# RWKV input stage: sixteen modulation pieces fetched at once, norm to mix chunk by chunk with five outputs side by side, low-rank projections in plain fp32

## What is computed

```python
mod = silu(c) @ ada_w[0] + ada_b[0]            # 6 x 1024; shift and scale are the first two
hn  = rms_norm(x, g) * (1 + scale) + shift
xx  = 0.5 * (x_prev + x_next) - hn             # neighbours of hn in the token direction
xs  = hn[:, :, None, :] + xx[:, :, None, :] * mu     # six mixes, j = 0..5
r, k, v = xs[0] @ w_rkv[0], xs[1] @ w_rkv[1], xs[2] @ w_rkv[2]       # 1024 x 1024 each
w  = tanh(xs[3] @ w1) ;  a = xs[4] @ a1 ;  g = sigmoid(xs[5] @ g1)   # low rank: 2x64, 2x64, 2x128
kk = k * k_k ;  kk = kk / max(sqrt(sum over the head of kk^2), 1e-12)
# then the bidirectional recurrence over r, w, k, v, kk, a; then 17 more stages
```

## Time and profile before

| | us |
|---|---|
| median of 3 runs | 3714.63 (3710.47 to 3714.92) |
| the profiled execution | 3717.88 |
| its span | 3716.1 |
| PE / DVE / ACT / POOL busy | 3304.6 / 1478.5 / 1139.4 / 180.1 |
| mean granted TensorE clock | 0.942 of full |
| DMA | 623.98 MB, mean 168 GB/s |

### The profile page before, as it was taken

The page is one execution under the profiler, slowest core; times in us unless marked ns, Lnnn a source line. Parts: engine busy times, 40 slices in busy tenths (PEclk is TensorE's granted clock), DMA queues, the critical chain, the costliest instruction groups (busy, mean ns, idle before and its releaser), DMA issues. The chain is left out here.

```text
span 3716.1 us, 54738 instructions
## 1 busy us (share of the span) xinstructions
PE 3304.6 (89%) x24132; PEld 2544.8 (68%) x24132; DVE 1478.5 (40%) x2702; ACT 1139.4 (31%) x1787; POOL 180.1 (5%) x338
## 2 busy tenths in 40 slices
PE   4778887899899779997999988999989998898898
PEld 3767766555499664544777765777767876777898
DVE  3545555322344542224333234333243334325554
ACT  2434443221244331113222223222232223124443
POOL 1022220000000000000000000000000000000000
PEclk7888998899899989998999989999989998999899
DMA  5233332699666119993444413444322222212352
GB/s 213 91 121 107 124 121 109 251 421 421 265 238 238 54 53 420 421 421 127 159 153 152 161 61 114 149 176 159 119 80 85 102 85 108 68 46 102 137 185 100
DMA packets 106574, 623.98 MB, mean 168 GB/s; under 512 B 11744, under 2 KB 14176, under 8 KB 47968
## 3 DMA queue, kind: packets, MB, share of 16 engines
q1 hardware_dynamic: 69760, 485.62, 34.2%
q0 software_dynamic: 36576, 134.85, 10.1%
HBM read 619.37 MB, written 1.05 MB: 167 GB/s over the span
## 5 line engine op out<-in xcount | busy, mean ns | idle before, releaser
L334 PE MATMUL ps<-t,t 128*128 128x512 f32 (+1 forms) x3520 | 1252.0, 356 | 162.3 <-DVE t L449 73.5
L335 PE MATMUL ps<-t,t 128*128 128x512 f32 (+1 forms) x3520 | 1225.8, 348 | 0.0
L336 PE MATMUL ps<-t,t 128*128 128x512 f32 (+1 forms) x3520 | 1225.0, 348 | 0.0
L310 DVE TENSOR_TENSOR t<-t,t 128x1024 fp32r<-128x1024 f32 x452 | 550.7, 1224 | 823.9 <-ACT t L300 821.9
L334 PEld LDWEIGHTS ps<-t,t 128*128 128x128 f32 x3520 | 679.2, 193 | 287.8 <-issue 107.9
L335 PEld LDWEIGHTS ps<-t,t 128*128 128x128 f32 x3520 | 681.5, 194 | 83.9 <-issue 2.9
L336 PEld LDWEIGHTS ps<-t,t 128*128 128x128 f32 x3520 | 680.0, 193 | 85.6
L300 ACT ACTIVATE t<-t 128x1024 fp32r<-128x1024 f32 x452 | 473.7, 1054 | 630.6 <-PE ps L336 611.1
L1047 PE MATMUL ps<-t,t 128*64 128x512 f32 x1248 | 302.6, 595 | 9.7 <-DMA t<-in_experts_dram 9.7
L1047 PEld LDWEIGHTS ps<-t,t 128*64 128x64 f32 x1248 | 120.2, 137 | 183.3 <-issue 147.7
L547 POOL DMA_DIRECT2D t<-in_wmod_dram x240 | 126.8, 534 | 1569.2 <-PE ps L498 1567.1
(11 more groups left out here) (291 smaller groups left out, 3042.8 us busy)
## 6 DMA issues: line engine op xcount, KB each, us to landing
t<-in_experts_dram SPq DMA_DIRECT2D x234, 1024.0 KB, 13.5
t<-in_wall_dram SPq DMA_DIRECT2D x221, 1024.0 KB, 4.9
t<-in_wmod_dram POOLq DMA_DIRECT2D x240, 512.0 KB, 5.8
t<-in_wall_dram SPq DMA_DIRECT2D x10, 512.0 KB, 3.6
t<-in_lora_dram POOLq DMA_DIRECT2D x8, 512.0 KB, 3.9
t<-in_rcst_dram POOLq DMA_DIRECT2D x1, 1536.0 KB, 6.5
t<-in_x_dram SPq DMA_DIRECT2D x1, 1024.0 KB, 12.4
t<-in_ctx_dram POOLq DMA_DIRECT2D x1, 1024.0 KB, 5.9
```

The costliest lines, as they stand in the source:

```text
L310: e.tensor_tensor(lo, self.raw(n), hi, ALU.subtract).then_inc(*net.wlo.up((self.name, n)))
L334: e.matmul(out, lh, rh, start=start, stop=False, **kw)
L335: e.matmul(out, lh, rl, start=False, stop=False, **kw)
L336: return e.matmul(out, ll, rh, start=False, stop=stop, **kw)
```

## The change

- *Fetches.* GpSimd issues pieces 0 to 15 at once; pieces 4 to 15 go into tensors that are not yet in use (r, k, v, kk, oacc, xx), each with a semaphore. SyncE sends vec and x first, then cst and rows, and starts the weight ring only when piece 12 has landed. ACT waits for vec and x only, PE for cst and rows. PE does the modulation steps in the order 0, 2, 1, 4, 3, 6, 5, 7.
- *Norm to mix.* For each chunk: norm (DVE), shift (ACT), neighbours' sum (now GpSimd), xx and mix 0 (DVE), high part (ACT), low part (DVE); weights are split in between. PE keeps five outputs open in five banks; output x joins at chunk 0, 1, 2, 4, 6 and catches up. Five weight buffers instead of three, two of them in the ring of modulation pieces, so later pieces wait until output 24 of PE is reached. Mixes 1 to 5 are made two chunks at a time, between outputs.
- *Low rank.* The four last outputs use plain fp32 matmuls, 8 each, straight from the ring and from unsplit mixes in places of their own: 32 instead of 96.
- *Keys.* Scaling, square, sum over heads, root and reciprocal move from the start of the recurrence to the end of this stage; the first lora load too.

The diff, cut:

```diff
     def pool_step(self, e, w, s):
         n = s // 2
         if s % 2 == 0:
-            for i in range(4 if n else 8):
-                self.fetch(e, w, 4 * n + 4 * (n > 0) + i)
+            for i in range(EARLY) if n == 0 else range(4 * n + 4, 4 * n + 8) if n > 2 else ():
+                self.fetch(e, w, i)
 
     def fetch(self, e, w, i):
+        net = self.net
         if i >= len(self.specs):
             return
-        if i >= NM:
-            w.wait_ge(*self.net.sums.of(("mod rows", i - NM)))
-        e.dma_start(self.at(i), self.net.wmod[i]).then_inc(self.net.s_mring[i % NM], 16)
+        if i >= EARLY:
+            w.wait_ge(*net.sums.of("mods room"))
+            w.wait_ge(*net.sums.of(("mod rows", i - NM if i >= EARLY + NM else i % NM)))
...
     def sp(self, e, w):
         a = self.args
-        for d, s in ((self.cst, a["cst"]), (self.vec, a["vec"]), (self.rows, a["rows"]), (self.XW[:, :, 0:256], a["x"])):
-            e.dma_start(d, s).then_inc(self.s_in, 16)
+        e.dma_start(self.vec, a["vec"]).then_inc(self.s_vec, 16)
+        e.dma_start(self.XW[:, :, 0:256], a["x"]).then_inc(self.s_x, 16)
+        e.dma_start(self.cst, a["cst"]).then_inc(self.s_in, 16)
+        e.dma_start(self.rows, a["rows"]).then_inc(self.s_in, 16)
+        w.wait_ge(self.s_early[8], 16)
...
+    def mixed(self, w, j, k):
+
+        vecs = self.net.vecs
+        w.wait_ge(*vecs.of(("mix low", j, k if j == 0 else k // 2) if j < 3 else ("mix", j, k // 2)))
...
+    def pe_side(self, e, w):
+        net, ws = self.net, self.ws
+        wts, bs, done = [], [], [0] * self.SIDE
+        for k in range(8):
+            for x in range(self.SIDE):
+                if k < self.JOIN[x]:
+                    continue
+                if len(wts) == x:
+                    wts.append(ws.pe(w))
+                    bs.append(net.banks.take(w, ("rkv", x)))
+                self.mixed(w, 0, k)
+                for c in range(done[x], k + 1):
+                    m = mm3(e, net.ps[:, bs[x], 0:256], both(wts[x], c), net.U(c, 0, 256), c == 0, c == 7)
+                done[x] = k + 1
+                if k == 7:
+                    m.then_inc(*net.sums.up(("rkv", x)))
+                    ws.used(x)
 
...
+        w.wait_ge(net.s_in, 32)
         self.norm.pe(e, w)
+        for s in (0, 2, 1, 4, 3, 6, 5, 7):
+            net.mods.pe_step(e, w, s)
+        net.bg_pe.s = 8
+        self.pe_side(e, w)
+        for n in range(self.SIDE, 24):
+            j = n // 8
+            o = 256 * (j % 2)
+            wt = ws.pe(w)
+            b = net.banks.take(w, ("rkv", n))
+            for k in range(8):
+                self.mixed(w, j, k)
+                m = mm3(e, net.ps[:, b, 0:256], both(wt, k), net.U(k, o, o + 256), k == 0, k == 7)
+            m.then_inc(*net.sums.up(("rkv", n)))
+            ws.used()
+            if n % 8 == 7:
+                net.sums.note(("mix used", j))
+        net.sums.note("mods room")
+        b = net.banks.take(w, "key lengths")
+        for p in range(8):
+            w.wait_ge(*net.acts.of(("key squares", p // 2)))
+            o = COFF["HS"][0] + 16 * p
+            m = e.matmul(net.ps[0:16, b, 0:256], net.cst[:, o:o + 16], self.squares[:, p, :], start=(p == 0), stop=(p == 7))
+        m.then_inc(*net.sums.up("key lengths"))
+        for n in range(24, 28):
+            j = min(n - 24, 2)
+            b = net.banks.take(w, ("rkv", n))
+            w.wait_ge(*net.landed(self.raw[j]))
+            wt = net.ring_at(self.raw[j])[:, HW * (n // 27):HW * (n // 27) + HW]
+            for k in range(8):
+                self.mixed(w, 3 + j, k)
+                m = e.matmul(net.ps[:, b, 0:256], col(wt, k), self.mix(3 + j)[:, k, :], start=(k == 0), stop=(k == 7))
+            m.then_inc(*net.sums.up(("rkv", n)))
...
+        for c in range(9):
+            if c < 8:
+                self.norm.act_apply(e, w, c)
+            if c:
+                self.act_high(e, w, 0, c - 1, 1)
+            if 1 < c < 7:
+                w.wait_ge(*net.sums.of(("mod rows", NM - 1)))
+                ws.act_to(e, w, c - 1)
+        for n in range(24):
+            j, o = n // 8, n % 8
+            if j < 2 and o < 4:
+                self.act_high(e, w, j + 1, o, 2)
+            ws.act_to(e, w, n + self.SIDE)
+            self.act_out(e, w, n, (net.r, net.k, net.v)[j][:, o, :], ACT.Copy)
+            if n > 19:
+                q = n - 20
+                w.wait_ge(*net.vecs.of(("key scaled", q)))
+                w.wait_ge(*net.sums.of(("mix used", 1)))
+                e.activation(self.squares[:, 2 * q:2 * q + 2, :], net.kk[:, 2 * q:2 * q + 2, :], ACT.Square).then_inc(
+                    *net.acts.up(("key squares", q)))
+        w.wait_ge(*net.sums.of("key lengths"))
+        e.activation(net.kinv[0:16, :], net.ps[0:16, net.banks.of("key lengths"), 0:256], ACT.Sqrt).then_inc(*net.acts.up("key lengths"))
+        net.banks.emptied("key lengths", net.acts, "key lengths")
+        for x, (dst, fn) in enumerate(((net.wT, ACT.Tanh), (net.aT, ACT.Copy), (net.gT[:, 0, :], ACT.Sigmoid), (net.gT[:, 1, :], ACT.Sigmoid))):
...
+        self.norm.dve_gain(e, w)
+        for c in range(10):
+            if c < 8:
+                self.norm.dve_scaled(e, w, c)
+            if 0 < c < 9:
+                x = c - 1
+                w.wait_ge(*net.pools.of(("beside", x)))
+                e.scalar_tensor_tensor(out=self.xx[:, x, :], in0=self.xx[:, x, :], scalar=0.5, in1=self.H(x),
+                                       op0=ALU.mult, op1=ALU.subtract).then_inc(*net.vecs.up(("shift", x)))
+                self.dve_mix(e, w, 0, x, 1)
+            if c > 1:
+                self.dve_low(e, w, 0, c - 2, 1)
+            if 2 < c < 8:
+                ws.dve_to(e, w, c - 2)
+        for n in range(24):
+            j, q = n // 8, n % 8
+            if q < 4:
+                self.dve_mix(e, w, (1, 2, 4)[j], q, 2)
+            elif j:
+                self.dve_mix(e, w, (3, 5)[j - 1], q - 4, 2)
+            if n > 19:
+                w.wait_ge(*net.acts.of(("rkv", 9 + 2 * (q - 4))))
+                c = slice(2 * q - 8, 2 * q - 6)
+                e.tensor_tensor(net.kk[:, c, :], net.k[:, c, :], net.vc("k_k", 2 * q - 8, 2).unsqueeze(2).to_broadcast([128, 2, 256]),
+                                ALU.mult).then_inc(*net.vecs.up(("key scaled", q - 4)))
+            ws.dve_to(e, w, n + self.SIDE)
+            if j < 2 and 0 < q < 5:
+                self.dve_low(e, w, j + 1, q - 1, 2)
+        w.wait_ge(*net.acts.of("key lengths"))
+        e.tensor_scalar(net.kinv[0:16, :], net.kinv[0:16, :], 1e-12, None, ALU.max).then_inc(*net.vecs.up("length"))
+        w.wait_ge(*net.vecs.of("length"))
+        e.reciprocal(net.kinv[0:16, :], net.kinv[0:16, :]).then_inc(*net.vecs.up("length over"))
...
+        net.bg_pool.go(e, w)
         w.wait_ge(*net.vecs.of("shift room"))
+        for c in range(8):
+            w.wait_ge(*net.acts.of((self.norm.name, "kept", c)))
+            e.tensor_tensor(self.xx[:, c, :], hp[:, c, 0:256], hp[:, c, 2:258], ALU.add).then_inc(*net.pools.up(("beside", c)))
+        net.stages[1].fetch(e, w, 0)
+        net.bg_pool.until(e, w, 2)
```

More of the change, by code:

```diff
@@ L774 @@
 class RwkvIn(Stage):
+    SIDE = 5
+    JOIN = (0, 1, 2, 4, 6)
     def __init__(self, net, i):
@@ L802, in pe @@
     def pe(self, e, w):
         net, ws = self.net, self.ws
-        net.input_ready(w)
+        w.wait_ge(net.s_in, 32)
         self.norm.pe(e, w)
-        net.bg_pe.until(e, w, 2)
-        n = 0
-        for j in range(6):
-            for o in range((8, 8, 8, 1, 1, 2)[j]):
-                wt = ws.pe(w)
-                b = net.banks.take(w, ("rkv", n))
-                w.wait_ge(*net.vecs.of(("mix low", j)))
-                rhs = self.rhs(j)
-                for k in range(8):
-                    m = mm3(e, net.ps[:, b, 0:256], both(wt, k), rhs[k], k == 0, k == 7)
-                m.then_inc(*net.sums.up(("rkv", n)))
-                ws.used()
-                n += 1
-            net.sums.note(("mix used", j))
@@ L865, in dve, with dve_low @@
+    def dve_low(self, e, w, j, q, n):
+        net, o, c = self.net, 256 * (j % 2), slice(q * n, q * n + n)
+        w.wait_ge(*net.acts.of(("mix high", j, q)))
+        e.tensor_tensor(net.UL[:, c, o:o + 256], net.oacc[:, c, :], net.UH[:, c, o:o + 256], ALU.subtract).then_inc(
+            *net.vecs.up(("mix low", j, q)))
     def dve(self, e, w):
@@ L877, in dve @@
-        w.wait_ge(*net.vecs.of("beside"))
-        e.scalar_tensor_tensor(out=xx, in0=xx, scalar=0.5, in1=hp[:, :, 1:257], op0=ALU.mult, op1=ALU.subtract).then_inc(
-            *net.vecs.up("shift"))
-        self.dve_mix(e, w, 0)
-        for j in range(6):
-            if j < 5:
-                self.dve_mix(e, w, j + 1)
-            for o in range((8, 8, 8, 1, 1, 2)[j]):
-                ws.dve(e, w)
-    def pool(self, e, w):
-        self.net.bg_pool.until(e, w, 2)
+        self.norm.dve_gain(e, w)
@@ L1488, in pe @@
         net.banks.rot = list(range(8))
```

(9 more changed lines are left out.)

190 lines of the change are left out of this document (91 added, 99 removed).

## The result

| | before | after |
|---|---|---|
| median | 3714.78 (4 runs) | 3670.71 (4 runs, 3662.45 to 3679.92) |
| ratio | | 0.9881, 95% interval 0.9860 to 0.9902 |
| profiled execution / its span | 3717.88 / 3716.1 | 3662.45 / 3660.7 |
| mean granted clock | 0.942 | 0.950 |

What follows compares the result with a forecast made beforehand. First stage bound in turn by DMA and modulation rows, a DVE/ACT chain with PE idle 26.2 us, then PE from 73.5. Gains 13.9 + 22.3 + 15.3 = 51.5 us give 3663 us; own range 3655 to 3674, with rivals 3647 to 3680.

Steps and rivals of the forecast that it cites:

- Up to G: Kernel start to the norm's first application (mark G): 34.0 us against 47.96, gain 13.9, bounds 31.5 and 40.
- the landing of x, `cst` and `rows`: At the start: x landed at 11.3 us, cst to 12.6, rows landed 15.5; PE's squares start about 15.5, no gain.
- squares at 18 or more: Sign at the start: if PE's norm squares start at 18 us or more, the queue order was mis-priced.
- my second rival: Modulation pieces not there: sixteen not taken at once, or cst at 18 or later; norm at 40 to 43, 3669 to 3672; chance 0.10.
- G to V: Norm's first application to the 24th output's end (mark V): 84.0 us against 106.3, gain 22.3, bounds 77 and 91.
- Output 5: The sixth output, first after the five side by side, starts 30.0 us after the norm's first application.
- the meeting of DVE and GpSimd: In the chunk loop, DVE delayed by GpSimd's steps: 0.2 us for each of 8 chunks, 1.6, rounded to 2.
- the first rival: DVE and GpSimd exclude each other in the chunk loop: 5.8 us instead of 2, some 6 in all; 3669; chance 0.14.
- if DVE keeps up: In the 19 later outputs, old stalls between mixes go; DVE has 2.63 us of work against 2.84 where it mixes.
- V to M: 24th output's end to the recurrence's first modulation step (mark M): gain 15.3 us (12 to 17) of the old 35.5.
- PE's clock: Rival, slower: granted clock at its lower level through the whole stage; 60 us against 51.5 gained, 3723; chance 0.03.
- The third: Rival, more is gained: PE warm at the joins of the outputs, x and cst early; 3655; chance 0.12.

Runs made afterwards that it cites:

- again: The changed kernel, unaltered, measured and profiled once more: 3668.44 (5 runs), ratio 0.9865 (0.9839 to 0.9891) to the kernel before.
- experiment 1: Changed kernel with PE's squares waiting for cst alone (3661.11), ACT splitting the next weight before the next mix's high part (3659.96), or both (3666.49); also rerun unaltered.

## Why the prediction was right

**The sign, the range and the likeliest case** held: 3663 forecast, 3670.7 and 3668.4 measured, within 3647 to 3680 and within the forecast's own range (3655 to 3674). Its 51.5 us were 45.0 at M; the 6.5 us between are two terms mis-sized, by 3.2 and 3.3, both to the same side. That "again" lies 51.6 us under the kernel before of its series is chance: at M it had gained 43.0.

**Up to G: 10.7 us for 13.9.** That no piece is waited for was right: the last one landed at 29.85, forecast 30.2. The step that failed is the landing of x, `cst` and `rows`: 11.3 us and 15.5 were forecast, and x came at 15.7, `cst` at 18.4, `rows` at 19.8. With it the path was wrong: in the forecast G hangs on the last piece, here it hangs on the squares, with 11.3 us of PE's own chain from their end to G. Two errors in how x's packets pass nearly cancel. I let 550 of them pass before GpSimd's data start at 4.3 us, yet GpSimd's data start at 2.7 and 39 had passed by 4.3. But the 85 per us that I gave for the time after that hold only from 8 us on (88); from 4.3 to 8 us it was 185, so that 897 had passed by 10 us, where I had all of them. What was missing is the tail: I took a landing for the time when the mean engine is done, and it is that of the slowest share (fifteen of sixteen at 12.78, the last at 15.71). The sign that the prediction set for this, squares at 18 or more, came true. So did the cause in my second rival, `cst` at 18 or later, but at a smaller price than the 40 to 43 it gave for G.

**G to V: 87.3 us for 84.0.** Output 5 started at G + 30.1, forecast G + 30.0, but by two errors that cancel: the meeting of DVE and GpSimd costs 7 x 0.41 = 2.9 us, not 2, a quarter of the way to the first rival (5.8), and other parts were a little shorter. That the mark fits so well is luck. The 3.3 us by which G to V is longer than its forecast lie behind it, and the step that failed is the overlap: "if DVE keeps up" was checked by DVE's sum of work (2.63 against 2.84), and the round over DVE and ACT was not; it takes 4.27 (experiment 1), until the five weights' lead is rebuilt. Turning two instructions of ACT's queue gives 3.5 us back.

**V to M: 20.2 us for 20.2.** 3.63 for the lengths beside the squares and 14.08 for 32 plain matmuls, 0.44 each, as the row from late in the kernel had it (0.43 in the earlier trace rows). The gain of this part is 18.1 and not 15.3, and that of G to V less by the same 2.8, because of the mark; the step that failed there is a count of outputs read off the last rows of a timeline instead of counted in a window.

**The other rivals.** PE's clock was not low through the stage: 0.67 in 34 to 60 us, 0.97 from 60 to 120. The third, more gained, didn't come about: x and `cst` were late. Nothing behind M took the gain back.

## What to carry to other kernels

When a stage's critical chain goes through two engines in turn, add up the round and not each engine's own work; an order within one queue can cost more than an idle engine. A large prefetch shares the DMA engines with every other load, and a load has landed only with its slowest share; so what is urgent and moves in small packets should be ahead of it in time. But holding the prefetch back until that has landed lets the queues run empty and makes the last piece late, which here gave the gain back. Two loads that count up one semaphore can't be told apart by its steps. Read the parts of a small gain from marks in the trace where later stages scatter by more than the gain.

## What the runs showed of the hardware

- From 8 to 10 us the two queues got the same number of packets, 88 per us each, with 1 KB in one and 3.6 KB on average in the other: 0.09 and 0.31 MB per us. From 4 to 6 us it was 385 against 90.
- Sixteen transfers of 512 KB were issued on GpSimd's queue in 0.53 us each without a wait; when the last one was issued (9.8 us), two had landed.
- x landed 13.6 to 16.4 us after its issue in seven kernels with the same sixteen pieces queued; with two pieces ahead, 8.7 and 8.4. In the kernel after fifteen of the sixteen steps of its semaphore were there 2.9 us before the last.
- A DVE instruction of 0.42 us takes 0.83 when it starts 0.16 us into GpSimd's sum of 0.71, both reading SBUF.
- The same 7,384 matmuls took 363 to 382 us, with the granted clock at 0.96 to 0.88.
- PE's matmuls on pieces that arrive every 1.28 us took 0.64 us per piece at first and 1.08 later, with a clock of 0.65 in that window.
